# Small experts computed in unsplit float32 in two 64-column tiles of TensorE, and their matrices taken one after the other

## What is computed

```python
logits = (t @ w_router).astype(jnp.float32)
top_vals, top_idx = lax.top_k(logits, TOP_K)          # 2 of 8
...
for e in range(N_EXPERTS):
    out = out + gates[:, e:e + 1].astype(t.dtype) * swiglu(t, w_gate[e], w_up[e], w_down[e])
def swiglu(t, w_gate, w_up, w_down):
    return (jax.nn.silu(t @ w_gate) * (t @ w_up)) @ w_down
```

## Time and profile before

| | |
|---|---|
| median of three runs | 1126.3 us (1125.69 to 1126.73) |
| the profiled execution, its own time | 1126.51 us |
| its span, first to last instruction | 1124.7 us |
| TensorE (PE) busy | 1101.6 us, 98% |
| VectorE (DVE) busy | 877.7 us, 78% |
| ScalarE (ACT) busy | 749.8 us, 67% |
| mean granted TensorE clock | 0.999 of 2.4 GHz |
| moved by DMA | 294.94 MB, mean 262 GB/s |

### The profile page before, as it was taken

How to read it: one execution, slowest core, us unless ns; L and a number is a source line. 1 busy time by engine, 2 the same in 40 slices (tenths; PEclk the granted TensorE clock), 3 DMA queues, 4 the chain that set the end, 5 groups by cost and what they waited for, 6 DMA issues and landing times.

```text
span 1124.7 us, 15463 instructions
## 1 busy us (share of the span) xinstructions
PE 1101.6 (98%) x5470; PEld 927.3 (82%) x5470; DVE 877.7 (78%) x1053; ACT 749.8 (67%) x921; POOL 39.5 (4%) x84
## 2 busy tenths in 40 slices
PE   9999999999999999999999999999899999999996
PEld 8888877888888888888877888887688887888875
DVE  6568877765445456568877689999998999999997
ACT  6545767454444446456766457899978898988785
POOL 3002000000000001002001000000000000000000
PEclk9999999999999999999999999999999999999999
DMA  9765534687555354655535649999999999999993
GB/s 327 270 159 181 183 106 130 188 274 253 197 183 182 127 181 148 198 144 185 170 121 168 205 149 333 372 418 413 418 418 354 380 402 410 404 417 405 412 365 140
DMA packets 135496, 294.94 MB, mean 262 GB/s; under 512 B 25486, under 2 KB 50156, under 8 KB 134908
## 3 DMA queue, kind: packets, MB, share of 16 engines
q1 hardware_dynamic: 134016, 288.23, 71.4%
q0 software_dynamic: 960, 5.28, 1.2%
q10 hardware_dynamic: 444, 0.47, 0.1%
HBM read 292.90 MB, written 1.05 MB: 261 GB/s over the span
## 4 chain that ended last, share of the span: by engine, by line
PE 77%; DVE 17%; DMA 2%; ACT 2%; issue 2%; ACTq 0%; SPq 0%; DVEq 0%
PE bank L1827 22%; PE bank L1829 21%; PE bank L1828 21%; DVE w_lo L1602 11%; DVE w_lo_more L1602 3%; PE bank L2259 2%; PE bank L2260 2%; PE bank L2079 2%; PE bank L1873 1%; DMA raw<-in_moe_w_gate 1%; PE bank L2059 1%; PE bank L2067 1%; DVE hid_buf L1741 1%; PE bank L2242 1%; ACT w_hi L1022 1%
## 5 line engine op out<-in xcount | busy, mean ns | idle before, releaser
L1243 DVE TENSOR_TENSOR w_lo<-raw,w_hi 128x1024 fp32r<-128x1024 f32 (+4 forms) x141 | 238.0, 1693 | 135.2 <-ACT w_hi L772 134.4
L772 ACT ACTIVATE w_hi<-raw 128x1024 fp32r<-128x1024 f32 (+5 forms) x141 | 201.5, 1432 | 144.1 <-PE bank L1829 144.1
L1602 DVE TENSOR_TENSOR w_lo<-raw,w_hi 128x1792 fp32r<-128x1792 f32 (+3 forms) x148 | 286.6, 1965 | 10.5 <-ACT w_hi L1022 9.6
L1022 ACT ACTIVATE w_hi<-raw 128x1792 fp32r<-128x1792 f32 (+3 forms) x148 | 244.0, 1666 | 44.6 <-PE bank L1829 31.2
L1827 PE MATMUL bank<-w_hi,aT_hi 128*128 128x512 f32 (+1 forms) x592 | 238.3, 403 | 0.8 <-DVE w_lo L1377 0.7
L1829 PE MATMUL bank<-w_hi,aT_lo 128*128 128x512 f32 (+1 forms) x592 | 229.8, 388 | 0.0
L1828 PE MATMUL bank<-w_lo,aT_hi 128*128 128x512 f32 (+1 forms) x592 | 229.5, 388 | 0.0
L1827 PEld LDWEIGHTS bank<-w_hi,aT_hi 128*128 128x128 f32 x592 | 111.3, 188 | 22.9 <-DVE w_lo L1377 1.0
L1829 PEld LDWEIGHTS bank<-w_hi,aT_lo 128*128 128x128 f32 x592 | 111.1, 188 | 22.7
L1828 PEld LDWEIGHTS bank<-w_lo,aT_hi 128*128 128x128 f32 x592 | 111.3, 188 | 21.0
L1602 DVE TENSOR_TENSOR w_lo_more<-raw,w_hi_more 128x1792 fp32r<-128x1792 f32 (+3 forms) x50 | 96.8, 1942 | 4.6 <-ACT w_hi_more L1022 4.6
(11 more groups left out here) (339 smaller groups left out, 1796.8 us busy)
## 6 DMA issues: line engine op xcount, KB each, us to landing
raw<-in_moe_w_gate SPq DMA_DIRECT2D x128, 448.0 KB, 6.6
raw<-in_moe_w_up SPq DMA_DIRECT2D x128, 448.0 KB, 6.5
raw<-in_moe_w_down SPq DMA_DIRECT2D x112, 512.0 KB, 6.7
raw<-in_w_in SPq DMA_DIRECT2D x40, 768.0 KB, 4.3
raw<-in_dense_w_gate SPq DMA_DIRECT2D x22, 512.0 KB, 3.8
raw<-in_dense_w_up SPq DMA_DIRECT2D x22, 512.0 KB, 4.6
raw<-in_dense_w_down SPq DMA_DIRECT2D x11, 1024.0 KB, 4.9
raw<-in_w_in SPq DMA_DIRECT2D x20, 512.0 KB, 4.6
```

What stands on the lines that cost most here:

```text
L772: act.activation(dst, src, ACT.Copy).then_inc(hi_made[j], 1)
L1022: act.activation(split_of(hi_slot, m), raw_of(i, n), ACT.Copy).then_inc(e_hi_made, 1)
L1243: dve.tensor_tensor(dst, src, high, ALU.subtract).then_inc(lo_made[j], 1)
L1602: dve.tensor_tensor(split_of(lo_slot, m), raw_of(i, n), split_of(hi_slot, m).bitcast(F32), ALU.subtract).then_inc(e_lo_made, 1)
```

## The change

- Small experts are no longer split. The 64 tokens stand in `x_small` in float32 (high part plus low part, added by VectorE in `pair_lo`), and TensorE multiplies `raw` itself in float32. The two granules of a chunk, one for each half of the hidden columns, are multiplied side by side: one into partitions 0 to 63 of a bank, the other into partitions 64 to 127 (`whole_gate_up`). A down granule's two halves of 512 columns go side by side in the same way (`whole_down`).
- `fold`, `shift` and `add_folded` go; the memory of `fold` holds the transposed hidden values. A small expert's output is one 128 x 512 tile and not two.
- A small expert goes in one go: its 16 gates (step `k` even), its 16 ups (step `k + 1`), and right behind them its 14 downs. Where a large expert stands before it, the last 7 downs of the large one stand behind the first 6 gates (`GATES_FIRST`).
- Only large experts' granules take `w_hi` and `w_lo` slots; they are split up to 8 such granules ahead. A small expert's `raw` slot is free when TensorE has multiplied it (SyncE waits for `e_used`).
- `bring_back` of pair p - 1 moves from step 4p + 2 to step 4p + 1.

```diff
+GATES_FIRST = 6
+def step_work(k):
+    gate_up, down = [], []
+    if k < STEPS and is_small(k):
+        gate_up = [(("gate", "up")[k % 2], k // 2, c, half) for c in range(KC) for half in range(2)]
+    elif k < STEPS:
+        gate_up = [(matrix, k // 2, c, k % 2) for matrix in ("gate", "up") for c in range(KC)]
+    gate_up = list(enumerate(gate_up))
+    if k and not is_small(k - 1):
+        down = [(GU_N + c, ("down", (k - 1) // 2, c, (k - 1) % 2)) for c in range(HK)]
+    elif k < STEPS and is_small(k) and k % 2:
+        down = [(GU_N + half * HK + c, ("down", k // 2, c, half)) for half in range(2) for c in range(HK)]
+    first = GATES_FIRST if k < STEPS and is_small(k) and k % 2 == 0 else GU_N
+    return gate_up[:first] + down + gate_up[first:]
...
-        for q, n in enumerate((1, 5, 7, 11)):
-            BETWEEN[k + 2, n] = ("back", p - 1, q)
+            BETWEEN[k + 1, n] = ("back", p - 1, q)
...
+                            elif unsplit(RAW_BEFORE[i]):
+                                sp.wait_ge(e_used, RAW_BEFORE[i] + 1)
                             else:
                                 sp.wait_ge(e_lo_made, SPLIT_OF[RAW_BEFORE[i]] + 1)
...
-            def small_product(dst, x, b_hi, b_lo, start, stop):
-                pe.matmul(dst, x, b_hi, start=start, stop=False)
-                return pe.matmul(dst, x, b_lo, start=False, stop=stop)
...
+            def whole_gate_up(r, k, n):
...
+                for u in range(2):
+                    for half in range(2):
+                        last = pe.matmul(bank[(B_GATE if matrix == "gate" else B_UP)[u]][half * SMALL:(half + 1) * SMALL, 0:HN], tokens,
+                                         raw_of(i + half)[:, 0, u * HN:(u + 1) * HN], start=c == 0, stop=c == KC - 1, skip_group_check=True)
+                last.then_inc(e_used, 2)
...
+            def whole_down(r, k, n):
...
+                slots = hT_small[:, c * P + half * SMALL:c * P + (half + 1) * SMALL]
                 for u in range(2):
+                    last = pe.matmul(bank[B_Y[0]][u * SMALL:(u + 1) * SMALL, :], slots, raw_of(i)[:, 0, u * NB:(u + 1) * NB],
+                                     start=half == 0 and c == 0, stop=half == 1 and c == HK - 1, skip_group_check=True)
+                last.then_inc(e_used, 1)
```

More of the change, by code:

```diff
@@ new lines, with granule_width, matrix_of @@
+WORK = {(k, n): what for k in range(STEPS + 1) for n, what in step_work(k)}
+IN_ORDER = [(k, n) for k in range(STEPS + 1) for n, _ in step_work(k)]
+GRANULES = [(r, k, n) for r in range(ROUNDS) for k, n in IN_ORDER]
+SEQ = {g: i for i, g in enumerate(GRANULES)}
+PER_ROUND = len(IN_ORDER)
+LAST_DOWN = {WORK[at][1]: at for at in IN_ORDER if WORK[at][0] == "down"}
+ENDS_WITH = {at: e for e, at in LAST_DOWN.items()}
+def granule_width(n):
+    return HALF if n < GU_N else D
+def matrix_of(i):
+    return WORK[GRANULES[i][1:]][0]
@@ L170 @@
 SPLITS = []
 for i in range(0, len(GRANULES), 2):
-    SPLITS += [(i, 2)] if granule_width(GRANULES[i][2]) == granule_width(GRANULES[i + 1][2]) else [(i, 1), (i + 1, 1)]
+    both = [x for x in (i, i + 1) if not unsplit(x)]
+    SPLITS += [(i, 2)] if len(both) == 2 and granule_width(GRANULES[i][2]) == granule_width(GRANULES[i + 1][2]) else [(x, 1) for x in both]
 SPLIT_OF = {i + x: m for m, (i, n) in enumerate(SPLITS) for x in range(n)}
-def slot_history(slots):
-    return [i - slots if i >= slots else None for i in range(len(GRANULES))]
+W_ORDER = sorted(SPLIT_OF)
@@ L181 @@
+W_AT = {i: at for at, i in enumerate(W_ORDER)}
 H_SLOTS = (2, 3, 4, 5)
 def h_slots_read(r, slots):
[L186 to L198, removed]
+    return max(i for i in range(PER_ROUND * r, PER_ROUND * (r + 1)) if (i + RAW_SLOTS // 2) % RAW_SLOTS in slots) + 1
@@ new lines, with hidden_between @@
+RAW_BEFORE = [i - RAW_SLOTS if i >= RAW_SLOTS else None for i in range(len(GRANULES))]
+W_BEFORE = {i: W_ORDER[at - W_SLOTS] if at >= W_SLOTS else None for i, at in W_AT.items()}
+SPLITS_BEHIND = {}
+for m, (i, n) in enumerate(SPLITS):
+    last = i + n - 1
+    at = max(-1 if W_BEFORE[last] is None else W_BEFORE[last], last - W_SLOTS)
+    if at >= last // PER_ROUND * PER_ROUND:
+        SPLITS_BEHIND.setdefault(at // 2, []).append(m)
+BETWEEN = {}
+def hidden_between(k, *at):
+    for q, n in enumerate(at):
+        BETWEEN[n] = ("hidden", k, q)
@@ L201 @@
+for k in range(STEPS):
+    if not is_small(k):
+        hidden_between(k, (k + 1, 3), (k + 1, 5 if is_small(k + 1) else 9))
+    elif k % 2:
+        hidden_between(k, (k, GU_N - 1), (k, GU_N))
 for p in range(PAIRS_E):
@@ L1791, in between @@
                         b = B_X[TURN[what] % 2]
-                        if kind == "hidden" and m < STEPS - 1:
+                        if kind == "hidden" and not is_small(m):
                             hidden_lo_half(r, m, q, b)
+                        elif kind == "tokens_lo":
+                            pair_lo(r, m, q, b)
                         elif kind == "back":
```

400 lines of the change are left out of this document (176 added, 224 removed).

## The result

The changed kernel took **1135.97 us** (median of 4 runs, 1134.42 to 1137.3), the kernel before in the same session 1126.35 us (4 runs, 1125.69 to 1126.73): a ratio of 1.0086, 95% interval 1.007 to 1.0102. It is slower by 9.6 us where 1112 us was forecast, and lies outside the range. The profiled execution of the changed kernel took 1137.3 us, with a span of 1135.5 us and a mean granted clock of 0.992.

The account below looks back on a forecast made before the run. TensorE in large experts, VectorE in small ones and the transfers (418 GB/s) lay within a few per cent. Block by block, products ended 14.7 us earlier: 1126.5 - 14.7 = 1111.8, so 1112 us; range 1104 to 1124.

Parts of the forecast that it names:

- The prediction's own signs of being wrong: Clock under 0.95 in small blocks, passes over 0.42 us, large experts late, transfers under 405 GB/s, SyncE waiting for TensorE.
- slow tiles: Small experts' float32 products on TensorE run slower than the attention's rows say: 1150 to 1290 us, chance 0.13.
- Part 1: Small experts' products on TensorE: two tiles share the time of one, 36.0 us an expert for 40.8 before.
- Its clause on the clock: TensorE's clock falls to half in small experts' products on few rows that wait for transfers: 1284 us.
- Part 2: Splitting: ScalarE's 1.71 us and VectorE's 2.02 us for two granules go, for 230 of 368 granules.
- Part 3: Behind a small expert's last up, TensorE waits 2.9 us for the hidden values; bounds 1.8 and 6 us.
- Part 4: Changes of TensorE's tile form: 0.2 us for a job in between, 3.6 us a small block, 2.4 us last expert.
- Part 5: Slots held until multiplied: run-ahead 12 granules, not up to 20; costed at nothing, at most 5 us behind a large expert.
- the sum: Block by block, the later of TensorE and the transfers decides; products end at 1098.3 us, 14.7 us earlier.

Follow-up runs that it names:

- the kernel with both repairs: The changed kernel with 16 raw and 6 split slots, and 40 identity transposes where TensorE waits for a large expert's first split: 1120.67 us, ratio 0.9957.

## Why the prediction was wrong

| position, us | forecast | changed kernel | 16 raw and transposes |
|---|---|---|---|
| second large expert begins | 830.3 | 836.6 | 833.8 |
| small gates begin | 884.2 | 891.6 | 887.0 |
| last large expert begins | 988.3 | 1005.2 | 996.3 |
| last small gates begin | 1044.1 | 1064.0 | 1052.8 |
| products end | 1098.3 | 1123.6 | 1106.7 |

By blocks the 25.3 us between forecast and trace are 6.3 + 1.1 + 9.5 + 3.0 + 5.4. The prediction's own signs of being wrong came true: large experts beginning after 835 and 995 us (836.6 and 1005.2), transfers under 405 GB/s in the small blocks (398), with SyncE waiting for TensorE (120.1 and 35.5 us). Its chances had no place for this: the one case in which the kernel gets slower was slow tiles.

**Part 1 was right.** The tiles share the time of one, and passes of 448 columns are 0.38 us apart (0.375 forecast). From the kernel with 16 slots and transposes, where two slots' names keep the rows apart:

```profile
1053.17 0.54 PE L2314 MATMUL bank<-raw,x_small 128*64 128x448 f32 x1
1053.18 0.54 PE L2314 MATMUL bank<-raw_more,x_small 128*64 128x448 f32 x1
1053.55 0.54 PE L2314 MATMUL bank<-raw,x_small 128*64 128x448 f32 x1
1053.56 0.54 PE L2314 MATMUL bank<-raw_more,x_small 128*64 128x448 f32 x1
```

The rival of slow tiles fell with it. Its clause on the clock held in three places of the changed kernel: at the two waits of 5 us, and once within small experts' products, in the last one (granted clock 0.86 from 1100 to 1112 us), where waits of 0.42 and 0.51 us for transfers and of 1.34 and 0.73 us for the hidden values come close together. Four products took 1.52 us there and 1.08 us elsewhere, 14 took 4.01 us and 3.17 us in the kernel with both repairs: 1.3 us in all. In the second small block it was 1.00 from 890 to 995 us. In the Trainium skill the section "HAM oscillation — how this bites in real kernels" of "TensorE: Matmul & The Clock Gate" warns of products on few rows between waits for transfers. The two waits of 5 us agree with it, at a price of 2.9 us for both; but it has the clock fall between all bursts, and in this kernel's first two small blocks it stayed at 1.00.

**Part 2 was right** (the busy times above): neither engine bounds any longer.

**Part 3 was right**: 2.7 us from the last up (763.52 + 0.92) to the first down, 2.9 if the last pass is counted at 0.38 us and not at its modelled length:

```profile
763.52 0.92 PE L2310 MATMUL bank<-raw,x_small 128*64 128x448 f32 x4
764.49 1.16 DVE L1761 TENSOR_TENSOR hid_buf<-sg_buf,bank 128x448 f32<-128x448 f32 x2 [2.55 <-PE bank L2310]
765.79 0.63 PE L2275 MATMUL bank<-ident,hid_buf 128*128 128x128 f32 x4 [1.35 <-DVE hid_buf L1761]
766.46 0.60 ACT L1161 ACTIVATE fold<-bank 128x512 f32<-128x512 f32 x1 [13.68 <-PE bank L2275]
767.15 1.08 PE L2339 MATMUL bank<-raw,fold 128*64 128x512 f32 x4 [0.73 <-issue]
```

**Part 4 had the mechanism, and too small a size**: around a bringing back in the last expert, again with 16 slots and transposes, the first product comes 0.15 us late after two passes of 0.43, the second 0.34 us behind it and not 0.23, and the tiles 0.09 us late. That is 0.35 us for the job, where the term was 0.2. It decided nothing: the transfers were the later side in the small blocks, and the last expert took 53.9 us in this kernel, 54.2 forecast.

```profile
1099.74 1.08 PE L2343 MATMUL bank<-raw,fold 128*64 128x512 f32 x4
1100.75 0.51 PE L2272 MATMUL bank<-y_hi,selT 128*128 128x512 f32 x1
1101.09 0.39 PE L2272 MATMUL bank<-y_lo,selT 128*128 128x512 f32 x1
1101.41 1.94 PE L2343 MATMUL bank<-raw,fold 128*64 128x512 f32 x8
```

**Part 5 is the step that failed.** It costed a run-ahead of 12 in place of 20 "at nothing where the transfers are the later side (slots stand free)", with 5 us as its upper bound. And the sum then put the issue at 723.54, granule 56, from the kernel before into a kernel in which that issue can't happen. Granule 52 went at 718.93 in the kernel before and at 724.84 in the changed one, 5.9 us later. Granule 56 then landed at 734.7 us and not at 730.2, and the 84 behind it took 98.0 us and not 96.2: together the 6.3 us by which the second large expert began late. From TensorE's first gates on, the next large expert is 113.5 us away by the chain above, so the block is that long whatever the engines save. The same happens at the second change (9.5 us), and at the third, where the last granule lands at 1118.8 us and not at 1087.5 as I had it. All of the slots' loss was bounded at one change by 5 us; it came at each of three, and what TensorE caught up in between was nothing, for a large expert's 46 granules take it 53.9 us and the transfers 52.7.

The forecast also took 418 GB/s for the whole of both small blocks. No kernel here held it: the best had 399 on the mean, and its products end 8.4 us behind the forecast. For that part the lead still cut at each change (from up to 22 to 16) is the likely reason; SyncE still stops there (from 720.87 to 725.52 us), and the rate falls to 265 GB/s from 723 to 730 us and 238 from 885 to 890. No run had enough slots to close this, so it stays unproven.

## What to carry to other kernels

When a stage is taken out between a transfer and its use, ask who freed the landing buffer. Here the split was also what freed it, up to 8 granules ahead of TensorE. Without it the buffer waits for the product itself, in the order of issue, and the queue behind it stands still though other slots are free. Where work with much lead is followed by work with little, cost the change as a chain, from the first use that frees a slot through all that must still land, and compare it with the block's engine time.

## What the runs showed that I had not expected

- A wait of 5 us was enough to bring the granted clock from 1.00 to the lower level (products 0.37 us apart and not 0.20), for 3.3 us after the first and 5.7 us after the second (1005.18 to 1010.91); the waits of 1.35 and 0.73 us around the hidden values were not in the first two small blocks, and were in the last expert, where waits for transfers stood just ahead of them. But in the kernel with 16 slots and transposes the same two waits did lower it in the first small block, with no such wait ahead (0.81 from 765 to 770 us, 0.85 from 770 to 775); what decides it was not found. 40 transposes with no use hold the clock, and gained 2.9 and 4.8 us. Waits of 3.00 us went either way: with 16 gates copied the clock stayed at 1.00 (730 to 740 and 900 to 910 us), with 6 copied it was 0.76 from 900 to 910 us.
- The worth of slots is far from linear: 10 for 12 cost 26.8 us, 16 for 12 gained 13.2 us in the changed kernel and 1.0 us in the kernel before (both with 6 split slots); there 6 for 8 split slots cost 35 us, in the changed kernel 2.6 us.
